# Six channel tiles of a depthwise convolution as plain fp32 products on 32-row blocks

## The reference, cut to what matters

```python
def mixer_conformer_conv(x, w_pw1, b_pw1, w_dw, b_dw, ln_g, ln_b, w_pw2):
    h = x @ w_pw1 + b_pw1
    a, g = jnp.split(h, 2, axis=-1)
    h = a * jax.nn.sigmoid(g)
    h = causal_depthwise_conv(h, w_dw) + b_dw
    h = jax.nn.silu(layer_norm(h, ln_g, ln_b))
    return h @ w_pw2
```

## Time and profile before

| | us |
|---|---|
| median of 3 runs | 2546.01 |
| lowest, highest | 2543.43, 2546.31 |
| profiled execution, its own time | 2546.59 |
| span of the profiled execution | 2544.8 |
| TensorE busy in the span | 2520.1 |
| VectorE busy | 1955.3 |
| ScalarE busy | 1200.0 |

### The profile page before, as it was taken

How to read it: one execution, slowest core, us unless ns; L and a number is a source line. 1 busy time by engine, 2 the same in 40 slices (tenths; PEclk the granted TensorE clock), 3 DMA queues, 4 the chain that set the end, 5 groups by cost and what they waited for, 6 DMA issues and landing times. The chain is left out here.

```text
span 2544.8 us, 41246 instructions
## 1 busy us (share of the span) xinstructions
PE 2520.1 (99%) x17241; PEld 2314.1 (91%) x17241; DVE 1955.3 (77%) x2571; ACT 1200.0 (47%) x1960; POOL 1.4 (0%) x10
## 2 busy tenths in 40 slices
PE   9999999999999999999999999999999999999999
PEld 7899999889888899998898899998898999999888
DVE  6988999577454679995784479996677979999576
ACT  6775444436233254443362245444356766444335
POOL 0000000000000000000000000000000000000000
PEclk9999999999999999999999999999999999999999
DMA  5202333324322223333233224333222203333322
GB/s 156 73 12 92 113 103 108 103 88 128 95 92 91 84 89 103 107 101 108 82 101 97 94 67 123 103 108 107 92 91 93 66 26 97 103 107 102 108 82 76
DMA packets 267054, 240.10 MB, mean 94 GB/s; under 512 B 14908, under 2 KB 212852, under 8 KB 266740
## 3 DMA queue, kind: packets, MB, share of 16 engines
q1 hardware_dynamic: 266292, 236.94, 30.2%
q10 hardware_dynamic: 576, 0.52, 0.1%
HBM read 233.21 MB, written 2.10 MB: 92 GB/s over the span
## 5 line engine op out<-in xcount | busy, mean ns | idle before, releaser
L1786 DVE TENSOR_TENSOR w_lo<-raw,w_hi 128x1024 fp32r<-128x1024 f32 x287 | 345.4, 1222 | 266.0 <-ACT w_hi L1309 265.7
L1309 ACT CAST w_hi<-raw 128x1024 fp32r<-128x1024 f32 x287 | 294.8, 1045 | 372.8 <-DMA raw<-in_ffn_w_down_dram 104.1
L879 PE MATMUL psum<-h_hi,w_lo 128*128 128x512 f32 x872 | 341.4, 392 | 0.0
L881 PE MATMUL psum<-h_hi,w_hi 128*128 128x512 f32 x872 | 339.4, 389 | 0.0
L880 PE MATMUL psum<-h_lo,w_hi 128*128 128x512 f32 x856 | 333.2, 389 | 0.0
L1024 PE MATMUL psum<-a_hi,w_lo 128*128 128x256 f32 x1088 | 280.9, 286 | 6.6 <-DVE w_lo L1786 5.1
L1024 PE MATMUL psum<-a_hi,w_hi 128*128 128x256 f32 x1088 | 277.5, 284 | 0.0
L1190 PE MATMUL psum<-h_hi,w_hi 128*128 128x256 f32 x768 | 217.3, 283 | 0.0
L1191 PE MATMUL psum<-h_hi,w_hi 128*128 128x256 f32 x768 | 217.3, 283 | 0.0
L1024 PEld LDWEIGHTS psum<-a_hi,w_lo 128*128 128x128 f32 x1088 | 209.1, 192 | 8.7 <-DVE w_lo L1786 4.6
L1024 PEld LDWEIGHTS psum<-a_hi,w_hi 128*128 128x128 f32 x1088 | 209.3, 192 | 0.3
(11 more groups left out here) (362 smaller groups left out, 6494.3 us busy)
## 6 DMA issues: line engine op xcount, KB each, us to landing
raw<-in_ffn_w_gate_dram SPq DMA_DIRECT2D x176, 256.0 KB, 3.0
raw<-in_ffn_w_up_dram SPq DMA_DIRECT2D x176, 256.0 KB, 3.3
raw<-in_ffn_w_down_dram SPq DMA_DIRECT2D x176, 256.0 KB, 3.1
raw<-in_a_w_pw_dram SPq DMA_DIRECT2D x94, 256.0 KB, 3.1
raw<-in_ple_w_gate_dram SPq DMA_DIRECT2D x64, 256.0 KB, 3.2
raw<-in_b_w_in_dram SPq DMA_DIRECT2D x64, 256.0 KB, 3.0
raw<-in_c_w_in_dram SPq DMA_DIRECT2D x48, 256.0 KB, 2.9
raw<-in_b_w_out_dram SPq DMA_DIRECT2D x32, 256.0 KB, 3.1
```

What stands on the lines that cost most here:

```text
L879: pe.matmul(bank(grp.g, j), st_lo, mv_hi, start=(k == 0), stop=False, skip_group_check=by_tiles(grp))
L881: done = pe.matmul(bank(grp.g, j), st_hi, mv_hi, start=False, stop=(ku == last and a == UK - 1), skip_group_check=by_tiles(grp))
L1309: act.copy(hi_u[u % RING], raw_u[u % RING]).then_inc(hi_ready, 1)
L1786: dve.tensor_tensor(lo_u[u % RING], raw_u[u % RING], hi_u[u % RING].bitcast(F32), ALU.subtract)\
```

## The change

All of tiles 2 to 7 (`QUADS`) go to TensorE, in **four output phases**, as plain fp32 products, and VectorE keeps tiles 0 and 1. ScalarE copies each input tile into phase order, unsplit (`conv_by_phase`). A block is now 32 rows by 128 columns: four 32-column diagonals, cut from one table per tile of 37 such diagonals (`make_blocks` on VectorE, 3 zero ones at each end, in fp32). One step multiplies it with 128 columns, for each of four row groups `r` into a bank of its own; 34 steps do the 31 taps of four phases. Outputs of a phase land on 32 partitions, and copies from PSUM bring them to their channels and tokens directly: two row groups by ScalarE (`move`), two by VectorE (`move_low`; for the first two segments ScalarE does all four). The DMAs that turned phases are gone. Tile 7 is done in two halves of the tokens, so there are seven segments, in alternate groups of banks.

```diff
-TAPS_PE = 27
-K_SHARED = 6
-PHASED = ((4, 0), (5, 0), (3, K_SHARED), (6, 0))
+PHASES = 4
+ROWS = P // PHASES
+STEPS = TAPS_A + PHASES - 1
+BLOCKS = TAPS_A + 2 * (PHASES - 1)
+QUADS = (2, 3, 4, 5, 6, 7)
+SEGMENTS = ((0, None), (1, None), (2, None), (3, None), (4, None), (5, 0), (5, 1))
+VECTOR_MOVES = 2
+CENTRE_IN, CENTRE_AT = 3, 20
+STATS_AT = 18
...
-            def phase_tap(s, n, e):
-                at = e % 2 * (CW // 2) + e // 2
-                for w, x in ((0, 1), (1, 0), (0, 0)):
-                    for r in range(2):
-                        moving = conv_split(n, x)[r * TILE_ROWS:(r + 1) * TILE_ROWS, at:at + HALF]
-                        last = pe.matmul(phase_bank(s, n, r)[:, 0:HALF], block_pair(n, e, w, r), moving,
...
+            def quad_tap(s, i, e):
+                n, (v0, n_v) = SEGMENTS[i][0], segment_span(i)
+                for r in range(PHASES):
+                    moving = rows(conv_phases(n), r)[:, e % PHASES, e // PHASES + v0:e // PHASES + v0 + n_v]
+                    block = rows(tap_blocks(n), r)[:, e * ROWS:e * ROWS + P]
+                    last = pe.matmul(segment_bank(s, i, r), block, moving, start=(e == 0), stop=(e == STEPS - 1))
+                return last
...
             def conv_taps(s):
...
+                for i, (n, h) in enumerate(SEGMENTS):
+                    if i < 2:
+                        take_half(s.taps_g + i)
                     else:
+                        pe.wait_ge(moved_high, moved(s, i - 2))
+                        pe.wait_ge(moved_low, moved(s, i - 2))
+                    if i == CENTRE_IN + 1:
+                        pe.wait_ge(centre_saved, c + 1)
+                    pe.wait_ge(conv_phased, len(QUADS) * c + n + 1)
+                    pe.wait_ge(blocks_made, len(QUADS) * c + n + 1)
+                    for e in range(STEPS):
+                        last = quad_tap(s, i, e)
+                        if i == CENTRE_IN and e == CENTRE_AT:
                             centre(s)
+                        if i == LAST and e == STATS_AT:
+                            conv_stats(s, 0)
                     last.then_inc(taps_done, 1)
...
+            def conv_by_phase(s, n):
+                act.wait_ge(prod_ready, s.prod0 + QUADS[n] // 2 + 1)
+                act.copy(conv_phases(n), by_phase(conv_x[:, QUADS[n], :])).then_inc(conv_phased, 1)
+            def move(s, i):
+                act.wait_ge(taps_done, moved(s, i))
+                for y, out_of in moves(s, i, HIGH):
+                    last = act.copy(y, out_of)
+                last.then_inc(moved_high, 1)
+                if i < VECTOR_MOVES:
+                    for y, out_of in moves(s, i, LOW):
+                        last = act.copy(y, out_of)
+                    last.then_inc(moved_low, 1)
...
+            def make_blocks(s, n):
+                blocks, edge = tap_blocks(n).rearrange("p (k s) -> p k s", k=BLOCKS), PHASES - 1
+                taps = prm_taps(s).rearrange("p (k m) -> p k m", m=DT)[:, :, QUADS[n]:QUADS[n] + 1]
+                own.add(dve.memset(blocks[:, 0:edge], 0.0))
+                own.add(dve.memset(blocks[:, BLOCKS - edge:BLOCKS], 0.0))
+                dve.tensor_tensor(blocks[:, edge:edge + TAPS_A], many(rep[:, :], TAPS_A),
+                                  taps.broadcast_to([P, TAPS_A, ROWS]), ALU.mult).then_inc(blocks_made, 1)
+            def move_low(s, i):
+                dve.wait_ge(taps_done, moved(s, i))
+                for y, out_of in moves(s, i, LOW):
+                    last = dve.tensor_copy(y, out_of)
+                last.then_inc(moved_low, 1)
...
             def conv_norm(s):
...
+                move(s, LAST)
+                half_affine_pair(s, 0, 0)
```

More of the change, by code:

```diff
@@ L381, in tap_block @@
[L381 to L401, removed]
+        BLOCK_WORDS = BLOCKS * ROWS
@@ new lines, in moves, with moved, mean_bank @@
+        def moves(s, i, groups):
+            n, (v0, n_v) = SEGMENTS[i][0], segment_span(i)
+            y = by_phase(tiles(h_f32, CONV_Y + QUADS[n]))
+            return [(rows(y, r)[:, PHASES - 1 - j, v0:v0 + n_v], rows(segment_bank(s, i, r), j))
+                    for r in groups for j in range(PHASES)]
+        HIGH, LOW = (2, 3), (0, 1)
+        def moved(s, i):
+            return len(SEGMENTS) * (s.layer // 3) + i + 1
+        def mean_bank(s):
+            return bank(s.taps_g, 0, 2).rearrange("p (h s) -> p h s", h=2)[:, :, SEQ // PHASES:SEQ // PHASES + HALF]
@@ L403, in prm_taps, with square @@
+        def square(m):
+            return tiles(h_f32, m - TILES)
         def prm_taps(s):
@@ L916, in centre @@
             def centre(s):
+                pe.wait_ge(moved_high, moved(s, CENTRE_IN - 1))
+                pe.wait_ge(moved_low, moved(s, CENTRE_IN - 1))
                 pe.wait_ge(ysum_ready, s.layer // 3 + 1)
[L921 removed]
+                for h in range(2):
+                    last = pe.matmul(mean_bank(s)[:, h], ones_r[:, :], hcol(ysum, h), start=True, stop=True)
+                last.then_inc(centre_done, 1)
             def conv_stats(s, h):
+                pe.wait_ge(moved_high, moved(s, LAST - 1 + h))
                 pe.wait_ge(conv_sums, 4 * (s.layer // 3) + 2 * h + 1)
@@ new lines, in move_low, with centre_sum @@
+            def move_low(s, i):
[3 more added lines that the diff above has]
+                last.then_inc(moved_low, 1)
+            def centre_sum(s):
+                own.settle()
+                wait_moved(s, 0)
+                wait_moved(s, 1)
+                for m in range(2):
+                    own.add(dve.scalar_tensor_tensor(tiles(tmp, 4 + m), conv_tile(2 + m), conv_bias(s, 2 + m), conv_tile(m),
+                                                     ALU.add, ALU.add))
@@ L1937, in conv_sums_of @@
-                own.add(dve.tensor_tensor(both, y(0, 2), y(2, 2), ALU.add))
-                own.settle()
-                own.add(dve.tensor_tensor(both, both, y(4, 2), ALU.add))
+                dve.tensor_tensor(three(conv_tile(0, 2), 2), three(conv_tile(0, 2), 2), many(mean[:, :], 2), ALU.subtract)\
+                   .then_inc(z_ready, 1)
+                place_centred(s, 2)
                 place_centred(s, 3)
+                wait_moved(s, 2)
+                place_centred(s, 4)
+                dve.wait_ge(z_ready, z0 + 3)
```

459 lines of the change are left out of this document (149 added, 310 removed).

## The result

| | before | changed |
|---|---|---|
| median of the runs measured together, us | 2545.11 (n = 4) | 2567.32 (n = 4) |
| lowest, highest | 2543.43, 2546.31 | 2566.45, 2568.30 |
| profiled execution, its own time | 2546.59 | 2566.45 |
| its span | 2544.8 | 2564.7 |
| mean granted clock of TensorE in it | 0.999 | 0.984 |

The account below looks back on a forecast made before the run. TensorE's own queue, busy 99%, was taken as the bound. Products 54.2, wait 0.9 and tail 2.7 make 57.8 us against 65.6, -7.8 per layer, -15.5 for two: 2531 us, own range 2522 to 2541, with program order to 2638.

Parts of the forecast that it names:

- segments 0 to 4 and centre: First five segments of the convolution on TensorE, about 7.6 us each, with the centre products: 38.2 us in layer 0.
- wait ahead of segment 5: TensorE waits for VectorE to move segment 3's low rows out of the bank segment 5 wants: 0.9 us.
- segments 5, 6 and statistics: The two 64-column halves of tile 7, charged full slots, and the statistics products on TensorE: 16.0 us.
- tail gap: Before mixer_out: eight ScalarE copies of the last half add 1.9 us to the old 0.78 us gap, 2.7 us.
- stage: The whole convolution stage per layer: 54.2 + 0.9 + 2.7 = 57.8 us against 65.6 before.
- copies out of PSUM: Moves of segments: eight on VectorE in 1.7 us; on ScalarE 4.7, 2.3 and 1.9 us a segment.
- the 0.56 case: The forecast itself: four row groups run at once on TensorE, two slots of 0.1115 us per step; chance 0.56.
- program order: Rival: TensorE passes start in issue order, four slots per step, +52.2 us per layer, 2635 us; chance 0.27.
- thin overlap: Rival: starts thin out on TensorE, four products take 0.145 us, +15 us per layer, 2561 us; chance 0.08.
- If a segment takes over 9 us: First sign, named in advance, that the forecast is wrong; a 128-column segment on TensorE was expected at 7.6 us.
- The moves: Rival: row groups overlap, but PSUM copies cost more (16 in 9.6 us), so 2549 us, no change; chance 0.06.
- second sign of being wrong: The forecast is wrong if TensorE's taps wait on moves for more than 3 us per layer.

Follow-up runs that it names:

- e8: The changed kernel plus 26 unused full-height products between segment 4's last tap and the wait before segment 5; 2538.56 us, ratio 0.9973.
- e1: The changed kernel with VectorE copying segment 3 out of PSUM before it waits for ScalarE's squares; 2535.28 us, ratio 0.9968.
- e6: e1 with VectorE moving segment 6 before its second scale, and making the first remainder before adding that segment; 2532.84 us, ratio 0.9956.
- e11: e6 plus 28 unused products of ones by ones behind the last tap; 2532.07 us, ratio 0.9949.
- e5: The changed kernel, its wait before segment 5 kept, with segments 5 and 6 streaming all 128 columns instead of 64; 2542.99 us.
- e2: e1 with a gap ahead of segment 4: TensorE waits there for ScalarE's copies of segment 3; 2542.91 us.
- e10: e1 with three steps (six passes) issued to a row group before the next, instead of one; 2660.68 us.
- e12: e1 with four steps (eight passes) issued to a row group before the next, instead of one; 2766.13 us.
- e7: e1 with six steps (twelve passes) issued to a row group before the next, instead of one; 2994.38 us.
- e4: e1 with two steps (four passes) issued to a row group before the next, instead of one; 2536.68 us.

## Why the prediction was wrong, by its own steps

| step, layer 0 | forecast | changed | cause |
|---|---|---|---|
| segments 0 to 4 and centre | 38.2 us | 39.8 | segments of 7.70 to 7.95 for 7.58, 8.45 with the centre |
| wait ahead of segment 5 | 0.9 | 3.28 | eight copies 3.10 for 1.7; begun 1.45 late |
| segments 5, 6 and statistics | 16.0 | 30.25 | clock 0.50; 16.6 in e8 at 1.00 |
| tail gap | 2.7 | 3.00 | copies on ScalarE 2.17 for 1.9 |
| stage | 57.8 | 76.3 | |

*The step that failed* is one the prediction never took: it priced all seven segments by rows at a granted clock of 1.00, read from a kernel whose stage had no gap, and priced the new wait at its length. The wait's true price was its length plus everything behind it at half clock. e8 takes the idleness out and leaves the wait: 2538.6 us, inside the forecast's own range of 2522 to 2541. The clock is the 28.8 us between that and 2567.3. As a check by layer: segments 5, 6 and statistics lost 30.25 - 16.6 = 13.6 us; mixer_out starts at half clock in both kernels, for 5.7 us here and 5.3 in e8.

*The terms that were mis-sized* make the 7.6 us from 2531.0 to 2538.6. In e8 the stage takes 164.42 - 101.26 = 63.2 us, and as long in layer 3, 5.4 over the forecast: 1.2 in segments 0 to 4, 2.5 in the (filled) wait, 0.6 in segments 5 and 6, 1.1 in the tail. Of the 10.8 us in both layers 2.0 come back in mixer_out (181.4 us in both layers for 183.4 before), and 0.9 because the forecast started from 2546.0 where the kernel before measured 2545.1.

Most of it is the copies out of PSUM. I took 0.21 us from 128-partition rows of VectorE with four and two times the elements, and 0.29 for ScalarE from activations out of SBUF. The changed kernel shows 0.39 on both engines, start to start (lines 1789 and 1311, 32x128), and 0.27 to 0.28 for 32x64. Which difference from those rows makes them dearer (fewer partitions, outputs four words apart, for ScalarE also PSUM as the source) no run tells. The later start of the chain, 140.75 for 139.3, came from the squares: they were done at 138.3 where 136.8 was forecast, because segment 3 ended 0.7 us late (133.1 for 132.4) and the copies that stand ahead of them on ScalarE are dearer too (3.18 us for 2.3). So the wait of 3.3 us instead of 0.9 came mainly from copies at 1.4 and 1.8 times their price in two places of one chain, and it was what let the clock fall. (The chain also put the end of segment 4 at 140.1, where its own slots give 101.4 + 38.2 = 139.6; it came at 140.7.)

The tail has a second cause that the forecast left out. In e8 it isn't ended by ScalarE's copies, which were priced, but by VectorE's eight. They begin 1.5 us behind the last tap (160.64), because VectorE is still at the norm's reciprocal and scales, for which the forecast's tail had no term (it took ScalarE's root and table loads to be over by then, as they are):

```profile
159.17 1.75 DVE L2007 RECIPROCAL rstd<-var 128x256 f32<-128x256 f32 x1
160.95 1.29 DVE L2015 TENSOR_TENSOR h_f<-h_f,rstd 128x512 f32<-128x512 f32 x2
162.16 2.21 DVE L1792 COPY h_f<-psum 32x64 f32<-32x64 f32 x8
```

In the changed kernel the taps were so slow that this chain was done in time, and its tail of 3.00 us looked nearly right.

*What was right.* Four row groups of plain fp32 passes share one slot (the 0.56 case): 7.70 us a segment, where program order would have given 15.2 and thin overlap 9.9. "If a segment takes over 9 us" therefore did not happen at full clock, and halves of 64 columns cost a full slot, as charged. None of the rivals is what happened, and none spoke of the clock. *The moves* came nearest: copies dearer than the nearest rows, with a price that e8 puts between forecast and rival (2531, 2538.6, 2549), had the clock not fallen. The second sign of being wrong that was named in advance, waits on moves of more than 3 us a layer, is what showed; it was named for the length of the waits, not for the clock.

Of rule and rows on the clock: the Trainium skill, "TensorE: Matmul & The Clock Gate", Part 1 "The HAM clock gate", says that TensorE's clock is throttled by default and activity lifts it. The gap that starts the fall agrees (e1 and e8 take the idleness away and it is gone). That a TensorE busy for 28.8 us stays at half clock is not what one reads out of it.

The best kernels found are e6 and e11, 2532.8 and 2532.1 us, 12 us less than before and 35 less than the changed kernel. Of these e6 does no useless work. It is the changed kernel with a few lines moved.

## What to carry to other kernels

A new wait on TensorE is to be priced twice: at its length, and at what stands behind it at half clock for as long as that work is thin; a gap of 3.3 to 3.5 us cost 3.8 us a layer ahead of 128-column products (e5, e2 against e1) and 16 us a layer ahead of 64-column ones (the changed kernel against e1). Here moving one early copy ahead of a wait removed the gap; filling it with products, or even doubling the columns behind it, gave the clock back too. And a small copy out of PSUM took 0.39 us where larger rows had led to 0.21: take its price from a row of the same shape, source and stride, not from a larger one scaled down. Look at the granted clock by stage before any busy share: TensorE is 99% busy in the kernel before and in the changed one.

## What the runs showed of the hardware that was not expected

- The same instructions can run at either clock, by the one at which they start. Four 64-column products of 32 rows per 0.11 us go on at 1.00 (e1, e8); begun at 0.50, where four take 0.2 us (224 in 11.5 us), they stay there, and the clock is down for 37.5 and 41.0 us. With 128 columns it was back 3.4 us after its fall (e2, e5).
- It can fall with no gap at all: with three, four or six steps per row group TensorE was 100% busy as it fell (e10, e12, e7), and it then stayed at 0.50 for 51, 109 and 290 us in layer 0.
- Across row groups TensorE reaches past three passes that stand behind the one at work, no further, as far as the starts tell (1, 3, 5 and 9 slots for groups of 4, 6, 8 and 12 passes in e4, e10, e12 and e7).
- Full-height products of 128 columns in the type fp32r start 0.11 us apart (56 in 6.47 us), hardly closer than those of 256 columns (26 in 3.38 us, 0.12); I had taken 0.056.
- What stays open: what in the stream makes the clock fall or come back, since columns, row groups at work and the rate of starts change together in these runs; and what decides whether a short gap lowers it.
